# Second block's output projection as seven block products, with weight and row sums made in place

## The reference

```
hn = rms_norm(x, norm_mix)
proj = hn @ w_in                                  # [256, 2336]
out_a = neighbourhood_attention(qa, ka, va, rpb)  # 6 heads, [256, 384]
out_b = mla_attention(qb, kb, vb)                 # 6 latent heads, [256, 384]
out_c = bc * conv(cc * hc)                        # [256, 256]
mixed = concat(rms_norm(out_a), rms_norm(out_b), rms_norm(out_c))   # [256, 1024], each with its gain
x = x + mixed @ w_out                             # [256, 1024] @ [1024, 1024]: the change
x = x + expert_choice_moe(rms_norm(x, norm_ffn))  # router, top 32 rows for each of 16 experts, width 1024
```

## Time and profile before

| | |
|---|---|
| median of 3 runs | 1926.46 us (1926.03 to 1927.03) |
| the profiled execution | 1926.92 us, span 1925.1 us |
| TensorE busy | 1643.8 us (85%) |
| VectorE busy | 764.6 us (40%) |
| ScalarE busy | 313.8 us (16%) |
| GpSimd busy | 182.2 us (9%) |
| DMA | 599.81 MB, mean 312 GB/s |
| chain that ended last | PE 55%, DMA 38%, DVE 4%, ACT 2% |

### The profile page before, as it was taken

The page is one execution under the profiler, slowest core; times in us unless marked ns, Lnnn a source line. Parts: engine busy times, 40 slices in busy tenths (PEclk is TensorE's granted clock), DMA queues, the critical chain, the costliest instruction groups (busy, mean ns, idle before and its releaser), DMA issues.

```text
span 1925.1 us, 25329 instructions
## 1 busy us (share of the span) xinstructions
PE 1643.8 (85%) x10768; PEld 941.6 (49%) x10768; DVE 764.6 (40%) x1502; ACT 313.8 (16%) x823; POOL 182.2 (9%) x175
## 2 busy tenths in 40 slices
PE   8999999999999999999776766757999785756757
PEld 3455999444589964574332232322474432232322
DVE  1586788877738886663010100102573010010101
ACT  1243111021521101262000000001252000010000
POOL 0001034000215410310000000000210000000000
PEclk9999999999999999999897987879999897897978
DMA  9992998434454743546999999999746999999998
GB/s 356 330 355 91 330 334 279 153 131 175 135 189 169 263 153 125 184 181 274 415 432 428 427 434 423 434 428 402 243 175 255 403 428 432 425 434 425 432 429 351
DMA packets 165960, 599.81 MB, mean 312 GB/s; under 512 B 20976, under 2 KB 79856, under 8 KB 142064
## 3 DMA queue, kind: packets, MB, share of 16 engines
q1 hardware_dynamic: 165630, 598.04, 79.2%
q10 hardware_dynamic: 242, 0.53, 0.1%
HBM read 594.76 MB, written 3.80 MB: 311 GB/s over the span
## 4 chain that ended last, share of the span: by engine, by line
PE 55%; DMA 38%; DVE 4%; ACT 2%; issue 1%; POOL 0%; SPq 0%; DVEq 0%; ACTq 0%; POOLq 0%
DMA extra<-in_w_down 14%; DMA extra<-in_w_up 13%; DMA extra<-in_w_gate 11%; PE ps L1393 7%; PE ps L1420 7%; PE ps L1747 5%; PE ps L1347 5%; PE ps L1018 4%; PE ps L1187 4%; PE ps L1464 4%; PE ps L1629 3%; PE ps L1289 3%; PE ps L1495 2%; PE ps L1767 1%; DVE extra L2548 1%
## 5 line engine op out<-in xcount | busy, mean ns | idle before, releaser
L1747 PE MATMUL ps<-ring,wide 128*32 128x256 f32 x2912 | 226.2, 478 | 123.9 <-DMA ring<-in_w_up 79.4
L1747 PEld LDWEIGHTS ps<-ring,wide 128*32 128x32 f32 x2912 | 109.5, 136 | 233.9 <-DMA ring<-in_w_up 89.0
L3446 DVE TENSOR_TENSOR wide<-ps,wide 128x512 f32<-128x512 f32 x16 | 10.7, 670 | 506.1 <-PE ps L1747 506.1
L1767 PE MATMUL ps<-ring,wide 128*32 128x512 f32 x768 | 158.4, 641 | 47.7 <-DMA ring<-in_w_down 44.0
L1747 PE MATMUL ps<-extra,wide 128*32 128x256 f32 x1056 | 87.1, 499 | 55.9 <-DMA extra<-in_w_up 31.8
L1767 PEld LDWEIGHTS ps<-ring,wide 128*32 128x32 f32 x768 | 42.2, 117 | 159.8 <-issue 127.6
L1393 PE MATMUL ps<-hT,ring 128*128 128x128 f32 x960 | 114.7, 275 | 0.0
L1393 PEld LDWEIGHTS ps<-hT,ring 128*128 128x128 f32 x960 | 111.0, 192 | 1.0 <-issue 1.0
L1347 PE MATMUL ps<-hT,ring 128*128 128x128 f32 (+1 forms) x704 | 100.2, 304 | 0.0
L2315 ACT ACTIVATE wide<-ps 128x512 f32<-128x512 f32 x8 | 4.8, 597 | 566.5 <-PE ps L1767 425.3
L1347 PEld LDWEIGHTS ps<-hT,ring 128*128 128x128 f32 x704 | 94.0, 191 | 5.8 <-issue 1.0
(11 more groups left out here) (399 smaller groups left out, 2364.5 us busy)
## 6 DMA issues: line engine op xcount, KB each, us to landing
ring<-in_w_gate SPq DMA_DIRECT2D x24, 4096.0 KB, 31.3
ring<-in_w_down SPq DMA_DIRECT2D x24, 4096.0 KB, 33.2
ring<-in_w_up SPq DMA_DIRECT2D x20, 4096.0 KB, 32.7
ring<-in_w_mod SPq DMA_DIRECT2D x24, 2048.0 KB, 12.9
ring<-in_w_up SPq DMA_DIRECT2D x44, 1024.0 KB, 9.5
extra<-in_w_gate SPq DMA_DIRECT2D x8, 4096.0 KB, 35.1
extra<-in_w_up SPq DMA_DIRECT2D x8, 4096.0 KB, 33.0
ring<-in_w_in SPq DMA_DIRECT2D x13, 2048.0 KB, 9.8
```

What stands on the lines that cost most here:

```text
L1747: last = mm(ps[2 * part + e // 2][j * CAP:(j + 1) * CAP, e % 2 * 2 * P:(e % 2 + 1) * 2 * P], xsT[:, k, e * CAP:(e + 1) * CAP], expert_row( ...
L1767: last = mm(ps[6 + n][e * CAP:(e + 1) * CAP, :], hidT[:, e, k, :], expert_row(n0, e, k)[:, n * N:(n + 1) * N], start=k == 0, stop=k == KD - 1)
```

## The change

```diff
+OUT2_STEPS = (1, 7, 2, 6, 3, 5, 4)
+OUT2_BANK = {1: 4, 7: 5, 2: 2, 6: 0, 3: 1, 5: 3, 4: 6}
+OUT2_SUMS = ("s3", "t3", "t2", "s1", "s2", "s4", "t4", "t1")
+OUT2_NEEDS = {1: (), 7: ("s3", "t3"), 2: (), 6: ("s2", "t2"), 3: ("s4",), 5: ("s1", "t1"), 4: ("t4",)}
...
+        def out2_weights():
+            v = [slot2(B2_AT[("out", n)]).rearrange("p (e g m) -> p e g m", e=2, g=4) for n in range(2)]
+            return [[v[n][:, e, :, :] for n in range(2)] for e in range(2)]
+        def out2_rows():
+            v = hT[:, :].rearrange("p (e g c t) -> p e c g t", e=2, g=4, c=2)
+            return [[v[:, e, c, :, :] for e in range(2)] for c in range(2)]
+        out2_s3 = spare[:, 2048:2560].rearrange("p (g t) -> p g t", g=4)
+        out2_u = sm[:, 2, :]
+        def out2_done(s, L, m):
+            if m == 4:
+                return tile_done, b2_used(L, B2_AT[("out", 1)])
+            return s.at("block_product_done", len(IN2_STEPS) + OUT2_STEPS.index(m))
+        def out2_sum(s, name):
+            return s.at("block_sum_ready", len(IN2_SUMS) + OUT2_SUMS.index(name) + 1)
...
-                def out2(bank, parts, c, n, some=slice(None)):
-                    wt = slot2(B2_AT[("out", n)]).rearrange("p (k n) -> p k n", k=KD)
-                    for k, at_, _ in parts[some]:
-                        last = mm(ps[bank][:, :], h8[:, at_, c * P:(c + 1) * P], wt[:, k, :],
-                                  start=k == parts[0][0], stop=k == parts[-1][0])
-                    return last
+                def block_out(m, some=range(4)):
+                    if some[0] == 0:
+                        for name in OUT2_NEEDS[m]:
+                            pe.wait_ge(*out2_sum(s, name))
+                    w, h = out2_weights(), out2_rows()
+                    lhs, rhs = {1: (h[0][0], w[0][0]), 2: (h[0][1], w[1][0]), 3: (h[0][1], w[1][1]), 4: (h[1][1], w[1][0]),
+                                5: (h[1][0], w[0][0]), 6: (h[0][0], w[0][0]), 7: (out2_s3, w[0][1])}[m]
+                    for g in some:
+                        last = mm(ps[OUT2_BANK[m]][:, :], lhs[:, g, :], rhs[:, g, :], start=g == 0, stop=g == 3)
+                    if some[-1] == 3:
+                        if m == 4:
+                            last.then_inc(tile_done, 2)
+                        else:
+                            last.then_inc(s.up("block_product_done"), 1)
                 for n in range(2):
                     pe.wait_ge(*b2_loaded(L, B2_AT[("out", n)]))
                 pe.wait_ge(*s.at("b2_out_by_act", 2))
                 pe.wait_ge(*s.at("b2_out_by_dve", 1))
-                out2(4, NEAR, 0, 0).then_inc(s.up("b2_out_done"), 1)
-                pe.wait_ge(*s.at("att_out_read", MAPS2))
+                block_out(1)
+                block_out(7, range(0, 2))
+                pe.wait_ge(*s.at("b2_mixed_ready", 2))
                 for i, (_, _, col) in enumerate(FAR):
                     for c in range(2):
                         o = ((i + 1) % 2) * T + c * P
                         last = nc.tensor.transpose(ps[6 + (i + 1) // 2][:, o:o + P], proj2[:, c, col:col + P], ident)
                     if i in (0, 2):
                         last.then_inc(s.up("b2_out_flipped"), 1)
-                out2(5, NEAR, 0, 1).then_inc(s.up("b2_out_done"), 1)
-                out2(0, NEAR, 1, 0).then_inc(s.up("b2_out_done"), 1)
-                out2(1, NEAR, 1, 1).then_inc(s.up("b2_out_done"), 1)
+                block_out(7, range(2, 4))
+                pe.wait_ge(*s.at("b2_proj_by_act", 7))
                 pe.wait_ge(*s.at("b2_out_by_act", 3))
                 pe.wait_ge(*s.at("b2_out_by_dve", 2))
-                out2(2, FAR, 0, 0).then_inc(s.up("b2_out_done"), 1)
-                out2(3, FAR, 0, 1).then_inc(s.up("b2_out_done"), 1)
+                block_out(2)
+                block_out(6)
+                block_out(3)
...
-                        pe.wait_ge(*s.at("b2_mixer_added", 2 * c + hf + 1))
+                        pe.wait_ge(*s.at("b2_mixer_added", (1, 2, 4, 3)[2 * c + hf]))
...
-                out2(6, FAR, 1, 0, slice(0, 2))
-                flip_rows(0)
-                out2(6, FAR, 1, 0, slice(2, 3)).then_inc(tile_done, 1)
-                out2(7, FAR, 1, 1, slice(0, 2))
+                flip_rows(0, (0,))
+                block_out(5)
+                block_out(4, range(0, 2))
+                flip_rows(0, (1,))
+                block_out(4, range(2, 4))
                 pe.wait_ge(sems["router_loaded"], 16 + DEPTH)
                 pe.wait_ge(sems["pads_cleared"], 4)
                 pe.wait_ge(*s.at("b2_x_by_act", 3))
                 pe.wait_ge(*s.at("b2_x_by_dve", 3))
                 route(0).then_inc(s.up("b2_router_done"), 1)
-                out2(7, FAR, 1, 1, slice(2, 3)).then_inc(tile_done, 1)
+                flip_rows(1, (1,))
+                logits(0)
                 flip_rows(1, (0,))
-                logits(0)
-                flip_rows(1, (1,))
+                pe.wait_ge(*s.at("b2_x_by_act", 4))
+                route(1, range(4, KD), 1)
                 pe.wait_ge(*s.at("b2_x_by_dve", 4))
-                route(1, range(0, 4))
-                pe.wait_ge(*s.at("b2_x_by_act", 4))
-                route(1, range(4, KD)).then_inc(s.up("b2_router_done"), 1)
+                route(1, range(0, 4), 1).then_inc(s.up("b2_router_done"), 1)
...
+                act.wait_ge(*out2_done(s, L, 1))
+                av(out2_u, ps[OUT2_BANK[1]][:, :], ACT.Copy).then_inc(s.up("b2_proj_by_act"), 1)
...
-                def near_add(c, n):
-                    dve.wait_ge(*s.at("b2_out_done", 2 * c + n + 1))
-                    xv = x[:, c, n * N:(n + 1) * N]
-                    tt(xv, ps[4 - 4 * c + n][:, :], xv, ALU.add).then_inc(s.up(), 1)
-                def far_add(c, n):
-                    if c == 0:
-                        dve.wait_ge(*s.at("b2_out_done", n + 5))
+                xh = [[x[:, c, n * N:(n + 1) * N] for n in range(2)] for c in range(2)]
+                w, h = out2_weights(), out2_rows()
+                def far_scale():
+                    dve.wait_ge(*s.at("b2_mixed_rstd", 2))
+                    for c in range(2):
+                        v = proj2[:, c, CQ2:CQ2 + 384]
+                        ts(v, v, rsm[1][:, 3 * c + 2:3 * c + 3], None, ALU.mult)\
+                            .then_inc(s.up("b2_mixed_ready" if c else None), 1)
+                def rows3(name):
+                    if name == "s3":
+                        dve.wait_ge(*s.at("b2_out_by_act", 2))
+                    elif name == "s1":
+                        dve.wait_ge(*s.at("b2_out_by_act", 3))
                     else:
-                        dve.wait_ge(tile_done, b2_used(L, B2_AT[("out", n)]))
-                    xv = x[:, c, n * N:(n + 1) * N]
-                    stt(xv, ps[2 + 4 * c + n][:, :], rsm[1][:, 3 * c + 2:3 * c + 3], xv, ALU.mult, ALU.add)\
-                        .then_inc(s.up("b2_mixer_added"), 1)
+                        dve.wait_ge(*out2_done(s, L, {"s2": 1, "s4": 2}[name]))
+                    dve.wait_ge(*s.own())
+                    out_, p, q, op = {"s3": (out2_s3, h[0][0], h[1][0], ALU.subtract), "s1": (h[1][0], h[1][0], h[1][1], ALU.add),
+                                      "s2": (h[0][0], h[1][0], h[0][0], ALU.subtract),
+                                      "s4": (h[0][1], h[0][1], h[0][0], ALU.subtract)}[name]
+                    tt(out_, p, q, op).then_inc(s.up("block_sum_ready"), 1)
+                def weights3(name):
+                    if name == "t3":
+                        for n in range(2):
+                            dve.wait_ge(*b2_loaded(L, B2_AT[("out", n)]))
+                    else:
+                        dve.wait_ge(*out2_done(s, L, {"t2": 1, "t4": 2, "t1": 6}[name]))
+                        dve.wait_ge(*out2_sum(s, {"t2": "t3", "t4": "t2", "t1": "t4"}[name]))
+                    out_, p, q, op = {"t3": (w[0][1], w[1][1], w[0][1], ALU.subtract), "t2": (w[0][0], w[0][1], w[0][0], ALU.add),
+                                      "t4": (w[1][0], w[0][0], w[1][0], ALU.subtract),
+                                      "t1": (w[0][0], w[1][1], w[0][0], ALU.subtract)}[name]
+                    tt(out_, p, q, op).then_inc(s.up("block_sum_ready"), 1)
+                def product_add(m, c, n, name=None, op=ALU.add):
+                    dve.wait_ge(*out2_done(s, L, m))
+                    dve.wait_ge(*s.own())
+                    tt(xh[c][n], xh[c][n], ps[OUT2_BANK[m]][:, :], op).then_inc(s.up(name), 1)
+                def shared_add():
+                    dve.wait_ge(*out2_done(s, L, 6))
+                    dve.wait_ge(*s.at("b2_proj_by_act", 7))
+                    tt(out2_u, out2_u, ps[OUT2_BANK[6]][:, :], ALU.add).then_inc(s.up(), 1)
+                    dve.wait_ge(*s.own())
+                    for c, n in ((0, 1), (1, 1), (1, 0)):
+                        tt(xh[c][n], xh[c][n], out2_u, ALU.add).then_inc(s.up(), 1)
...
-                near_add(0, 0)
```

(43 more changed lines are left out.)

12 lines of the change are left out of this document (6 added, 6 removed).

## The result

The changed kernel takes **1916.31 us** (median of 5 runs, 1915.64 to 1918.68) against 1926.46 for the kernel before on the same chip: ratio 0.9950, 95% interval 0.9936 to 0.9964. A repetition in a second job gave 1917.34 against 1925.82, 8.5 us.

What follows compares the result with a forecast made beforehand. The projection was taken as TensorE-bound, the expert stage as transfer-bound, its stream restarted by issues behind the projection and the experts' start. Two layers of 2.87 us give 5.7 off the 1926.46 median: 1920.7 us, range 1918.2 to 1923.2.

Steps and rivals of the forecast that it cites:

- X: Move of the projection's end, and so of the weight pair's issue: 3.25 us earlier per layer.
- The bubbles: Two TensorE waits in the projection, 0.48 us before the far transposes and 0.27 us before product 2.
- GpSimd's first step: First step of the reciprocal root in the projection, held up by weight sum t3; to last about 1.6 us.
- D: Rival: GpSimd's root is not held up by the weight sum; 3.62 us gained per layer, 1919.2 us; chance 0.12.
- VectorE's covers: Spare time of VectorE's new work in the projection: 1.0 us before product 5, 0.7 us before the transposes behind it.
- A: Rival: VectorE is late by 1 to 2 us per layer in the projection; 1923.7 us; chance 0.10.
- C: Rival: VectorE is the bound, its in-place sums running longer beside TensorE's reads; 1931.9 us at 30% more; chance 0.04.
- B: Rival: transfers hide the gain, the stream being held by slots freed later in the expert stage; 1926.5 us; chance 0.04.
- the walk: Step-by-step timing of layer 0's projection on TensorE, VectorE and GpSimd, with shared sum and three adds ending at 883.5.
- the tail: Router behind the last projection product: VectorE's evacuation becomes last, second logits at +3.45 for +3.07, late by 0.38 us.
- Y: Move of the experts' start: 3.25 - 0.38 = 2.87 us earlier per layer, taken as what counts.
- The step that failed: Claim that 6 MB behind the pair land just before the row parts' issue, so the experts' start sets the stream's gain.

Runs made afterwards that it cites:

- `sum_early`: The changed kernel with the first weight sum, t3, made before the last heads' read-outs, where VectorE waits for TensorE; 1915.65 us, ratio 0.9946 to the kernel before.
- `cover_used`: The changed kernel with two more row sums on VectorE, results unused, ahead of t1, the weight sum product 5 needs; 1917.81 us, ratio 0.9958 to the kernel before.
- `pair_held`: The changed kernel with SyncE's issue of the weight pair held until the router's first product; 1920.41 us, ratio 0.9976 to the kernel before.
- `pair_early`: The kernel before with the last projection product ahead of the router's first product, so the weight pair is issued sooner; 1922.80 us, ratio 0.9990.
- padded: Kernels before and after, each with 14 unused one-column VectorE copies more per layer; 1928.35 us (ratio 1.0012) and 1922.17 us (0.9972).
- code moved: Kernels before and after, each with six unused matmuls more in layer 0's row selection, shifting code fetches; 1925.00 us (ratio 1.000) and 1917.51 us (0.9959).
- `before_again`: The kernel before, unchanged, profiled a second time; 1925.49 us, ratio 0.9995.

## Why the prediction was right and where it failed

**Right: the projection.** X was forecast as 3.25 us and is 30.04 - 26.68 = 3.36. The bubbles, 0.48 and 0.27, are 0.45 and 0.25 (the waits of the timelines of after and of `sum_early` set against each other). GpSimd's first step was forecast as about 1.6 and is 1.69. That t3 is what holds it up was an inference from one row; `sum_early` shows it: t3 away, 0.21. The rule of the Trainium skill on this (SBUF — State Buffer, section Who interferes with whom) holds here, with the sum beside the step (1.69 us) and without it (0.21), and D, the rival without it, is out. VectorE's covers of 1.0 and 0.7 us: 0.8 is there before product 5, and the transposes behind it do not wait. A and C did not come; `cover_used` shows that A's point was placed rightly, since 0.6 us beyond the cover became 0.6 us of delay of product 5. B is out: the expert stages got shorter on average, not longer. One sum of the walk is 0.3 us short (four operations of 0.69 us from 881.0 on end at 883.8, not 883.5); nothing hangs on it, as VectorE then waits for product 5 until 885.7.

**Roughly right: the tail.** Late by 0.38 us was forecast, 0.65 came (Q 12.51 against 11.86). The chain is the forecast one, VectorE's evacuation last, the exponential at +2.99 behind the start of the last add (886.96) and the router's copy behind it at +3.30. The last transposes start at +1.18 in place of +0.95: the first logits take 0.22 us of TensorE ahead of them, which the forecast named but gave no time. So Y is 2.71, not 2.87: 0.3 us of the total.

**The step that failed** is "The row parts are therefore what holds the stream, and Y counts; X beyond Y would only empty the queue earlier", and with it "the expert stage from there as long as before". It rested on 14.7 us for 6 MB, ready at 907.7, 0.3 us before the row parts' issue at 908.01. The trace of before has the sixth MB complete at 909.92: the first byte comes 1.03 us behind the pair's issue, which the sum left out, and the 6 MB (6.29 million bytes) took 15.86 us, 397 GB/s in place of the 427 of a full stage. The first 1.03 us do not decide, since no first row packet came less than 1.03 us behind its issue in the profiles of before and after, which is 909.04 here; the rate does, and 909.92 is 0.9 us behind that. So the transfers ahead filled the DMA engines until a row packet could come, the row parts held nothing up, and bytes moved with X. Only in after did the engines begin to run dry ahead of the row packets (share 0.65 against 0.98). In relation to the experts the 29th MB came 1.0 us earlier. That stream and time follow the pair is shown by `pair_held` (+1.0 us for the 29th MB, +2.9 in time) and `pair_early` (-0.9, and -2.6 in time, of which 0.8 are its shorter P + Q). The bound that I had given this, 0.38 per layer, was too small as well.

**The sum by stages.** The projections give 2.72 x 2 = 5.4. The expert stages of the four profiles each of before and after (with padded and code moved) have means of 435.32 and 432.07 in layer 0, 436.95 and 435.84 in layer 1: 3.25 + 1.11 = 4.4. Together 9.8, between the two measured differences of 8.5 and 10.15. Of the 4.4, some 2.0 are the stream's lead (1.0 per layer). The other 2.4 or so lie at the end of layer 0, where before has the longer wait for the last part (1.98 against 0.79 us on average, four profiles each) and in two of four profiles the lower clock behind it. No term of the prediction has this. That a shifted code fetch causes it was argued from packets, has a profile against it (`pair_early`) and was not confirmed by a time. It stays open, as does why the lead is larger than the pair's move.

## What to carry to other kernels

Whether a queue is empty when the next transfer is issued must be read from the packets, not worked out from a mean rate of another stretch: here 1.2 us of error from the rate, in a point that was 0.3 us away from deciding, turned the answer over, and a forecast that close should have had its other side in the range at full size. If VectorE has long sums with both inputs in SBUF, place them away from the short GpSimd steps on the path: moving one sum ahead shortened the stage by 0.84 us per layer, a third of what the change itself had brought there, though in the time of the whole kernel it can't be told. And compare stages that begin and end with the same work over several profiles before explaining a difference of spans: 2.7 of 11.0 us here were the start's chance.

## What was not expected of the hardware

- The start of one and the same kernel differs between executions: the first block's first matmul came at 24.36 and 26.53 us in two profiles of before.
- The first byte of the 4 MB pair came 1.03 to 1.07 us behind its issue, into DMA engines that had been all but idle (share 0.03 or less in the 2 us before), in all 14 profiles; that of the row parts 1.03 to 1.05 us behind theirs in after, and 1.24 to 1.41 in before.
- A single instruction fetch, 16 KB and 1.08 us in one packet, went with a last weight part that came 3.95 to 4.26 us behind the one before it in place of 2.65 to 2.73, in three profiles; in a fourth, `pair_early`, it did not. That the one caused the other is not shown.
- A wait of TensorE of 2.33 us was followed by a granted clock of 0.50 (1.2 GHz) in `before_again`, one of 2.25 us by 1.00 (2.4 GHz) in the first profile of before: eight records of matmuls in 1.77 us and in 1.06.
